# A two-block transformer kernel on one Trainium2 core: gate rows spread by DMA instead of by matmul, and the last attention heads' masks moved ahead in VectorE's queue

## What is computed

```python
c_act = jax.nn.silu(c)
mod = c_act @ ada_w[l] + ada_b[l]                    # 6 * 1024 values for the whole layer
shift1, scale1, gate1, shift2, scale2, gate2 = [...] # six rows of 1024
h = rmsnorm(x, norm1_g[l]) * (1.0 + scale1) + shift1
proj = h @ w_in[l]                                   # qa ka va fa qb kb vb ga gb
o_fox = forgetting_attention(qa, ka, va, log_f)      # 8 heads of 64
o_sb = stick_breaking_attention(qb, kb, vb)          # 8 heads of 64
merged = sigmoid(ga) * (o_fox @ w_branch_fox) + sigmoid(gb) * (o_sb @ w_branch_sb)
x = x + gate1 * (merged @ w_out[l])
h2 = rmsnorm(x, norm2_g[l]) * (1.0 + scale2) + shift2
x = x + gate2 * hierarchical_moe(h2, ...)            # 16 experts, 2 per token
```

## Time and profile before

| | |
|---|---|
| Time, median of 3 runs | 687.23 us (687.14 to 687.46) |
| The profiled execution's own time | 687.28 us |
| Its span in the profile | 685.5 us |
| PE busy | 674.8 us |
| DVE busy | 439.4 us |
| ACT busy | 328.0 us |
| Instructions | 9987 |
| Granted TensorE clock, mean | 0.999 of full |
| Moved by DMA | 201.68 MB |

### The profile page before, as it was taken

How to read it: one execution, slowest core, us unless ns; L and a number is a source line. 1 busy time by engine, 2 the same in 40 slices (tenths; PEclk the granted TensorE clock), 3 DMA queues, 4 the chain that set the end, 5 groups by cost and what they waited for, 6 DMA issues and landing times.

```text
span 685.5 us, 9987 instructions
## 1 busy us (share of the span) xinstructions
PE 674.8 (98%) x3856; PEld 478.6 (70%) x3856; DVE 439.4 (64%) x793; ACT 328.0 (48%) x547; POOL 0.2 (0%) x4
## 2 busy tenths in 40 slices
PE   8999999999999999999999999999999999999997
PEld 5999999777778888999877778875343344344334
DVE  6877967878968988687988588664323323323223
ACT  6744434755676669333656876432213223223123
POOL 0000000000000000000000000000000000000000
PEclk9999999999999999999999999999999999999999
DMA  8987776663357534676947653689999999999971
GB/s 348 418 333 301 304 279 272 226 239 124 124 200 291 184 119 190 246 270 264 381 191 261 260 207 131 247 338 416 431 419 418 425 421 430 412 426 423 422 316 62
DMA packets 22893, 201.68 MB, mean 294 GB/s; under 512 B 2754, under 2 KB 3522, under 8 KB 7876
## 3 DMA queue, kind: packets, MB, share of 16 engines
q1 hardware_dynamic: 22272, 200.22, 73.6%
q10 hardware_dynamic: 580, 0.91, 0.4%
HBM read 200.07 MB, written 1.05 MB: 293 GB/s over the span
## 4 chain that ended last, share of the span: by engine, by line
PE 94%; DVE 3%; ACT 1%; issue 1%; DMA 1%; SPq 0%; DVEq 0%; ACTq 0%
PE psum L997 19%; PE psum L998 18%; PE psum L999 18%; PE psum L1361 16%; PE psum L1379 8%; PE psum L1310 2%; PE psum L1330 2%; PE psum L1228 1%; PE psum L1208 1%; PE psum L1246 1%; DMA ring<-in_chunks 1%; PE psum L1231 1%; PE psum L1485 1%; PE psum L1249 1%; PE psum L1112 1%
## 5 line engine op out<-in xcount | busy, mean ns | idle before, releaser
L2139 DVE TENSOR_TENSOR ring_rounded<-ring,ring_rounded 128x1024 fp32r<-128x1024 f32 (+1 forms) x128 | 149.3, 1202 | 23.8 <-ACT ring_rounded L1714 23.7
L1714 ACT ACTIVATE ring_rounded<-ring 128x1024 fp32r<-128x1024 f32 (+1 forms) x128 | 126.3, 1035 | 6.9 <-PE psum L999 6.9
L997 PE MATMUL psum<-hT_rounded,ring_rounded 128*128 128x256 f32 x360 | 102.6, 285 | 0.2 <-DVE gate_rows L2058 0.2
L998 PE MATMUL psum<-work_rounded,ring_rounded 128*128 128x256 f32 x360 | 101.9, 283 | 0.0
L999 PE MATMUL psum<-hT_rounded,ring_rounded 128*128 128x256 f32 x360 | 101.8, 283 | 0.0
L1361 PE MATMUL psum<-ring,work 128*64 128x512 f32 x320 | 83.8, 592 | 0.0
L998 PE MATMUL psum<-ring_rounded,hT_rounded 128*128 128x512 f32 (+1 forms) x208 | 79.5, 382 | 0.0
L997 PE MATMUL psum<-ring_rounded,hT_rounded 128*128 128x512 f32 (+1 forms) x192 | 76.0, 396 | 0.3 <-ACT work L1632 0.3
L999 PE MATMUL psum<-ring_rounded,work_rounded 128*128 128x512 f32 (+1 forms) x192 | 73.1, 381 | 0.0
L997 PEld LDWEIGHTS psum<-hT_rounded,ring_rounded 128*128 128x128 f32 x360 | 69.1, 192 | 0.7 <-ACT work L1620 0.3
L998 PEld LDWEIGHTS psum<-work_rounded,ring_rounded 128*128 128x128 f32 x360 | 69.1, 192 | 0.1
(11 more groups left out here) (320 smaller groups left out, 1078.5 us busy)
## 6 DMA issues: line engine op xcount, KB each, us to landing
ring<-in_chunks SPq DMA_DIRECT2D x44, 2048.0 KB, 8.1
ring<-in_expert_w_down SPq DMA_DIRECT2D x16, 2048.0 KB, 14.5
ring<-in_expert_w_gate SPq DMA_DIRECT2D x24, 1024.0 KB, 12.9
ring<-in_expert_w_up SPq DMA_DIRECT2D x16, 1024.0 KB, 13.5
gates<-in_expert_w_up SPq DMA_DIRECT2D x8, 1024.0 KB, 18.6
hT<-in_expert_w_gate SPq DMA_DIRECT2D x4, 1024.0 KB, 14.3
mixed<-in_expert_w_gate SPq DMA_DIRECT2D x4, 1024.0 KB, 16.8
ring<-in_chunks SPq DMA_DIRECT2D x4, 512.0 KB, 7.6
```

Source lines behind the costliest of these rows:

```text
L997: nc.tensor.matmul(out, a[0], b[0], start=start, stop=False, skip_group_check=True)
L998: nc.tensor.matmul(out, a[0], b[1], start=False, stop=False, skip_group_check=True)
L1714: nc.scalar.activation(as_rounded(high_piece(c, q)), src[:, piece_of(c, q)], ACT.Copy).then_inc(chunk_hi, 1)
L2139: v.tensor_tensor(as_rounded(w[:, piece]), w[:, piece], was_rounded(high_piece(c, q)), ALU.subtract)\
```

## The change

It has two parts. First, the four mod units and their four copies go. In their place ACT issues two DMAs per gate: `gate_store` writes the 128 x 8 gate columns into a scratch row of 1024 floats in HBM, transposing on the way (element (p, c) goes to place 128 c + p), and `gate_row` waits for that store and loads the row into all 128 partitions of `gate_rows`. Store 0 stands between the high parts 1 and 2 of kb, row 0 after the eviction of `("fm", "qb", 0)`; store 1 stands after P 14, row 1 where the mod units 10 and 11 were. DVE waits for row 0 before the first `wout` eviction of block two, and for row 1 before the experts. Second, on DVE the two masks of P 15 are put in front of the low parts 2 and 3 of `("proj", "f")`, and the closing step of the two heads is a step of its own, `sticks`, behind these low parts.

```diff
     steps.append(("logf",))
     split_placed(kb, (0, 1))
-    unit("mod", 4)
+    steps.append(("gate_store", 0))
     split_placed(kb, (), (0,))
-    unit("mod", 5)
     split_placed(kb, (2, 3), (1,))
     unit("fm", "qb", 0)
+    steps.append(("gate_row", 0))
     split_placed(kb, (), (2,))
...
             turn = todo.pop(0)
             steps.extend(turn[:-1])
-            split_placed(f, (), (1, 2, 3))
+            split_placed(f, (), (1,))
             unit(*u)
             steps.append(turn[-1])
+            split_placed(f, (), (2, 3))
+            steps.append(("sticks", turn[-1][1]))
             heads(todo)
...
         if u == ("tm", "h2", 1):
+            steps.append(("gate_store", 1))
             steps.append(("y_split", "f"))
             split_placed(f, (0, 1))
...
         if u == ("tm", "h3", 1):
-            unit("mod", 10)
-            unit("mod", 11)
+            steps.append(("gate_row", 1))
             split_placed(sb, (0, 1))
...
+    gate_scratch = nc.dram_tensor("gate_scratch", (2, D), F32, kind="Internal").ap()
...
-                elif kind == "mod":
-                    c = u[1]
-                    pe.wait_ge(gate_cols_ready, 1 if c < N_MOD else 2)
-                    for j in range(ADA_TILES):
-                        last = nc.tensor.matmul(b[:, j * P:(j + 1) * P], mod[:, c, j:j + 1].to_broadcast([P, P]), ident,
-                                                start=True, stop=True)
...
+            def gate_store(i):
+
+                act_e.wait_ge(gate_cols_ready, i + 1)
+                with nc.allow_non_contiguous_dma(reason="few bytes"):
+                    act_e.dma_start(gate_scratch[i].rearrange("(c p) -> p c", p=P),
+                                    mod[:, GATE_CHUNKS[2 * i]:GATE_CHUNKS[2 * i] + 2, :].rearrange("p c j -> p (c j)"))\
+                     .then_inc(gate_cols_stored, 16)
+
+            def gate_row(i):
+
+                act_e.wait_ge(gate_cols_stored, 16 * (i + 1))
+                act_e.dma_start(gate_rows[:, i, :], gate_scratch[i:i + 1, :].to_broadcast([P, D])).then_inc(gate_row_loaded, 16)
...
-                elif kind == "mod":
-                    c = u[1]
-                    last = v.tensor_copy(gate_rows[:, c // N_MOD, (c % 2) * W512:(c % 2 + 1) * W512], b[:, :])
...
                         dve.wait_ge(dve_evicted, evict_count(u) - 1)
+                        dve.wait_ge(gate_row_loaded, 16)
...
-                for h in pair:
+                for h in pair if p < 15 else ():
                     s, st = score[:, h % 2, :], hstat[:, h % 2, :]
                     dve.wait_ge(exp_done, h + 1)
...
+            def stick(h):
+
+                z = soft[:, h % 2, :]
+                v.scalar_tensor_tensor(z, score[:, h % 2, :], 0.0, z, ALU.max, ALU.add).then_inc(probs_ready, 1)
+
+            def sticks(p):
+
+                for h in (2 * p, 2 * p + 1):
+                    dve.wait_ge(exp_done, h + 1)
+                    stick(h)
...
+            dve.wait_ge(gate_row_loaded, 32)
             dve.wait_ge(onehot_ready, 1)
             combined(0, 0, 0, True)
```

More of the change, by code:

```diff
@@ L674, in two_block_kernel @@
         gate_cols_ready = sem("gate_cols_ready")
+        gate_cols_stored = sem("gate_cols_stored")
+        gate_row_loaded = sem("gate_row_loaded")
         sumsq_ready = sem("sumsq_ready")
@@ L1761, in _ @@
                     xn_scaled(s[1], s[2])
+                elif s[0] in ("gate_store", "gate_row"):
+                    (gate_store if s[0] == "gate_store" else gate_row)(s[1])
                 elif s[0] in ("norm_half", "sigmoid", "split", "y_split", "fa_split", "load_final_g"):
@@ L2204, in probs @@
                     else:
-                        z = soft[:, h % 2, :]
-                        v.scalar_tensor_tensor(z, s, 0.0, z, ALU.max, ALU.add).then_inc(probs_ready, 1)
+                        stick(h)
[5 more added lines that the diff above has]
+                    dve.wait_ge(exp_done, h + 1)
+                    stick(h)
             def turned(p):
@@ L2344, in _ @@
                     n += 1
-                elif s[0] not in ("begin", "residual", "xn", "S", "split", "y_split", "sigmoid", "load_final_g"):
-                    dict(square=square, roots=roots, c_rows=c_rows_silu, ada=ada, gate_cols=gate_cols, norm_half=norm_half, weighted_half=weighted_half, split_low=split_low, y_split_low=y_split_low, fa_split=fa_split, norm=norm, x1=x1, P=probs, T=turned, V=outputs, pool=pool, mods=mods, logf=logf,
+                elif s[0] not in ("begin", "gate_store", "gate_row", "residual", "xn", "S", "split", "y_split", "sigmoid", "load_final_g"):
+                    dict(sticks=sticks, square=square, roots=roots, c_rows=c_rows_silu, ada=ada, gate_cols=gate_cols, norm_half=norm_half, weighted_half=weighted_half, split_low=split_low, y_split_low=y_split_low, fa_split=fa_split, norm=norm, x1=x1, P=probs, T=turned, V=outputs, pool=pool, mods=mods, logf=logf,
                          scale_router=scale_router, picks=picks, scale=scale, route=route, slots=slots, weigh=weigh, xn_lo=xn_lo)[s[0]](*s[1:])
```

## The result

The kernel after takes **691.67 us** (median of 6, 691.07 to 692.79), the kernel before 687.22 beside it (687.03 to 687.46): a ratio of 1.0066, 95% interval 1.0056 to 1.0077. Slower by 0.7%. The forecast was 683.9 in a range of 683.2 to 687.6: wrong in sign, and outside its range.

The account below looks back on a forecast made before the run. The prediction took PE to bound the kernel, busy 674.8 of 685.5 us. Its terms, -1.70 - 0.19 - 1.81 + 0.3 + 0.1 = -3.3 us, from the median 687.23 gave 683.9 us, range 683.2 to 687.6.

Parts of the forecast that it names:

- In such a kernel an instruction taken from PE gives its full time: PE is busy 674.8 of 685.5 us, so deleted matmuls count in full if nothing else is late.
- the first pair: Mod units deleted near 308 us: minus 1.70 us of PE, and minus 0.19 for a wait at 316.55.
- 0.3 and 0.1 put for ACT's costs: Losses in the sum: 0.3 us for issuing store 1 in a busy stretch, 0.1 for store 0 landing late.
- The second pair and the masks: Mod units deleted near 402 us: minus 1.81 us of PE, if the reordered masks let heads 30 and 31 keep up.
- Rival 1: Second pair gives little, low part 3 or head 31 being late by over 0.04 us: 685.4 us, chance 0.12.
- The tightest meeting: Around T 15, head 31's closing step ends at 405.26 where PE wants it at 405.30: 0.04 us to spare.
- Row 1 and store 1 at no cost: Store 1, issued at 394 into idle DMA, is awaited by row 1 only after 404: that wait costs nothing.
- When store 0 is issued: After the second of kb's four high parts on ACT, at 312.3, leaving 7.0 us until it must be down.
- landed at 319.9 against 319.8: Store 0's forecast landing against the time row 0 needs it, with 0.9 us for completion; put at 0.1 us.
- the turns packet by packet: Store 0 alternates with 0.59 us weight packets: 6 of 64 through by 317.4, the other 58 in 1.6 us.
- The bounds that I took, 4.9 and 9.8 us: Earlier ACT DMA landing times, taken for store 0: landed at 317.2 or 322.1, a cost of 0 or 2.3 us.
- Rival 3: Store 0 runs into the next weight chunk if packets exceed 66 ns: 688.7 us at 70 ns, 700 at 100; chance 0.14.

Follow-up runs that it names:

- Experiment 1: The kernel after with row 0 (its wait for store 0 and its load) moved behind the eviction of h0 0, over 10 us later on ACT: 683.61 us.
- experiment 6: The kernel after, but ACT stores the numbers 512 bytes apart at store 0's place and waits for that; real store 0 and row 0 come later: 683.62 us.
- experiment 2: Experiment 1 with a store of 128 32-byte runs at store 0's place, awaited where row 0 stood; the real store 0 issued only then: 686.45 us.

## Why the prediction was wrong

- **"In such a kernel an instruction taken from PE gives its full time":** right. Experiment 1 shows 2.16 us for the first pair (forecast 1.89), 3.80 at T 15 (forecast 3.4), 3.8 at the end (forecast 3.3, with 0.3 and 0.1 put for ACT's costs).
- **The second pair and the masks:** right, also in the kernel after. Its T 15 starts at 410.45, 4.2 us after that of the earlier trace rows, while it was 3.4 (scores) + 2.4 (clock) = 5.8 behind: 1.6 of the 1.81 came in. Rival 1 did not happen. The tightest meeting had more room than the 0.04 us of the forecast: in experiment 1 head 31's closing step ends at 402.97 for a PE that takes it at 403.30 (402.44 + the 0.86 to its second head, as in the earlier trace rows).
- **Row 1 and store 1 at no cost:** right. Store 1 landed 12.2 us after its issue at 399.32, and ACT's wait of 1.5 us held no PE. It was as late as store 0, though; it cost nothing because of its place. (Row 1 landed some 74 us before DVE's first read at 494.6, not over 80.)
- **When store 0 is issued:** wrong, and made good by luck. I put it behind two high parts, at 312.3. ACT issued it at 310.19, before the high parts that stand ahead of it in the list had run: in these runs a DMA issue with no semaphore between them doesn't wait for the queued ACTIVATEs. So the store had 9.6 us until 319.8 and not 7.0. But its first packet was taken only at about 313.9, 3.7 us after the issue, where I had 1.4 (store 1, with no stream beside it, needed 0.9). The two errors cancel to my 313.7.
- **The failed step is the completion of store 0**, 0.9 us in "landed at 319.9 against 319.8". Its terms, one by one. The count of packets is right. So are the turns packet by packet: 80 packets, 5 for each engine, were through by 317.2 (forecast 6 by 317.4), and the 60 left for each engine took 1.8 us, to 319.0 (forecast 58 in 1.6, to 319.0). The busy time of one, 9 ns (28.0% of 16 x 2 us for 965), is not the 27 I took, but in this stretch they came 30 ns apart. What was missing is the end: I gave "start and completion" 0.9 us each, from a landing of whole rows, and the completion alone took 6.1 us (packets gone by 319.0, landed at 325.1). For the spread pieces of experiment 6 the 0.9 holds: gone by 319.0, landed at 319.9, which is the forecast's own number. In the sum this is the term of 0.1 us: the store was 5.3 us late, and that cost 7.9 with the clock. The bounds that I took, 4.9 and 9.8 us, were landings of long runs; the upper one was no bound for neighbouring 4-byte writes (14.9). That nothing in the trace was of the kind was written, and yet the two nearest rows were taken as ends. Why the completion of such writes is slow stays open.
- **Rival 3** had the right side and place, ACT held at row 0 with PE behind it, at 0.14, and the wrong mechanism: it needed 66 ns a packet and the next chunk as a competitor, and the packets were gone 1.9 us before that chunk was issued at 320.92. Its form of price also left out the clock: a stall of 5.5 us cost 7.9.
- **The page of the Trainium skill cited against the store,** "DMA: Bandwidth & Descriptors": its rule on a strided last dimension (Rules for kernel authors) was right to speak against it, and in its count of one descriptor for each element; the runs put the cost not in their number but in where they point. With its turns of some 9 to 17 descriptors (Queues, rings and completion order) the trace doesn't agree: 74 packets of the store beside 77 of the stream in 314 to 317 are turns of one, and the landing near 317 that I drew from them did not follow.

## What to carry to other kernels

A transpose on the way to HBM by 4-byte pieces is late by its completion, not its packets: give it more than the 16.1 us that was the longest here before its reader, keep weight loads that are soon needed out of its wake, or let the pieces start 16 bytes apart or more where the reader can bear it (no run here loads a row back from such a spread one). Put the DMA that waits for another DMA where nothing urgent stands behind it in its engine's order; here one moved line turned +4.4 us into -3.7. And when a deletion shortens one engine, look for what would be late next: the masks' reorder was worth 1.5 us only beside the deletion.

## What the hardware showed that was not expected

- 128 numbers of 4 bytes side by side in HBM land after 8.3 to 10.1 us, 512 after 7.7, 1024 after 9.1 to 16.1 (the change's own stores among them): the lateness hardly grows with the number, so a price for each piece can't be read from it. 1024 pieces at 8 bytes apart take 5.4 us, from 16 bytes on 2.7 to 3.2.
- Beside the weight stream a store's 4-byte packets and the stream's of 16 KB alternate one for one (74 and 77 in 314 to 317).
- Such a store holds other queues. Experiment 1 and the kernel before, in the same stretches, the second of which the next chunk should fill:

```profile
320.00:324.00 4.00, 4.00 (x36) 3.54 (x35) 3.20 (x10) 1.16 (x4) 0.00 (x0) 1.00 1.23 57
324.00:331.00 7.00, 7.00 (x63) 6.75 (x61) 6.35 (x14) 5.69 (x11) 0.00 (x0) 1.00 0.59 220
```

```profile
320.00:324.00 4.00, 4.00 (x36) 3.54 (x35) 2.55 (x5) 0.60 (x1) 0.00 (x0) 1.00 0.36 66
324.00:331.00 7.00, 7.00 (x61) 7.00 (x60) 6.27 (x18) 4.24 (x11) 0.00 (x0) 1.00 0.95 400
```

  Issued 1.4 us earlier than before, the chunk still moved at 220 in place of 400 GB/s. In experiment 1 no engine waited for it; in experiment 2 ACT did. Store 1 does the same there: the expert loads issued from 398.72 moved at 20 to 33 GB/s until 403, and at 389 in 405 to 406, after it had landed at 403.7. In the kernel before, such loads issued at 400.87 were at 377 in 403 to 404.
- Towards the end of PE's pause of 5.3 us the granted clock fell (0.80 in 324 to 325), was 0.50 until 331, and cost 2.4 us on top.
